# Plain fp32 products for layer 0's projections in a new order, and five changed joints between stages, in a two-layer encoder kernel

## What is computed

```python
for l in range(2):
    xn = rmsnorm(x, norm1_g[l])
    cq, ckv, k_rope, u, gate_a, gate_b = split(xn @ w_in[l])   # 256, 128, 32, 512, 1024, 1024 columns
    gate_a, gate_b = sigmoid(gate_a), sigmoid(gate_b)
    attn = mla(cq, ckv, k_rope)       # latent attention, 8 heads, q and k RMS-normed per head
    branch_a = attn @ w_attn_up[l]
    y = s5_bidir(u, ...)              # diagonal complex state space, 32 groups of 16 channels, both directions
    z = gelu(y) @ w_glu[l]
    branch_b = z[..., :1024] * sigmoid(z[..., 1024:])
    x = x + (gate_a * branch_a + gate_b * branch_b) @ w_o[l]
    x = x + (silu(rmsnorm(x, norm2_g[l]) @ w_ffn_gate[l]) * (rmsnorm(x, norm2_g[l]) @ w_ffn_up[l])) @ w_ffn_down[l]
```

## Time and profile before

| what | value |
|---|---|
| median of 3 executions | 1662.17 us (1661.73 to 1666.11) |
| profiled execution, its time | 1664.14 us |
| profiled execution, span of the trace | 1662.4 us |
| granted TensorE clock, mean | 0.969 |
| PE busy | 1544.8 us (93%) |
| DVE busy | 907.0 us (55%) |
| POOL busy | 587.1 us (35%) |
| ACT busy | 565.2 us (34%) |

### The profile page before, as it was taken

One profiled execution on the slowest core, in us unless ns is written; L12 is line 12 of the kernel. 1 busy time (PEld: TensorE's weight loads), 2 busy tenths in 40 slices (PEclk: granted clock), 3 DMA queues, 4 the chain that ended last, 5 costly groups with the idle time before them and its releaser, 6 DMA issues.

```text
span 1662.4 us, 21281 instructions
## 1 busy us (share of the span) xinstructions
PE 1544.8 (93%) x8488; PEld 1269.3 (76%) x8488; DVE 907.0 (55%) x1247; ACT 565.2 (34%) x885; POOL 587.1 (35%) x285
## 2 busy tenths in 40 slices
PE   6869598999999979999999799888999999999999
PEld 4757487777778858887888788777777788888887
DVE  7999677758645978683232643477593322112210
ACT  5322125663244222323232222467323322223220
POOL 3300013225444345433543322323344444444442
PEclk9979798999999989999999799999999999999999
DMA  5258650022233234535325462100332222222232
GB/s 183 89 170 283 212 216 19 2 77 92 86 107 111 76 127 149 198 95 167 104 99 181 170 238 71 64 1 27 102 99 79 90 101 98 93 90 91 98 102 76
DMA packets 73058, 188.36 MB, mean 113 GB/s; under 512 B 23552, under 2 KB 32000, under 8 KB 68864
## 3 DMA queue, kind: packets, MB, share of 16 engines
q1 hardware_dynamic: 35856, 124.99, 22.4%
q10 hardware_dynamic: 37104, 62.01, 11.3%
HBM read 154.47 MB, written 32.51 MB: 112 GB/s over the span
## 4 chain that ended last, share of the span: by engine, by line
PE 66%; DVE 19%; DVEq 5%; DMA 4%; ACT 3%; issue 2%; ACTq 1%; SPq 0%
PE ps L1413 21%; PE ps L1415 20%; PE ps L1414 20%; DVE mix L1356 2%; PE ps L1539 2%; DVE qkTl L1277 1%; DVE mix L1354 1%; DMA ctd_scr<-CPp 1%; DVE work L871 1%; DVE nmx L1310 1%; PE ps L1668 1%; ACT prob L783 1%; DMA y_scr<-SS 1%; PE ps L1677 1%; DVE work L872 1%
## 5 line engine op out<-in xcount | busy, mean ns | idle before, releaser
L392 POOL TENSOR_TENSOR wl<-stage,wh 128x1024 fp32r<-128x1024 f32 x215 | 538.7, 2510 | 930.4 <-ACT wh L456 930.3
L456 ACT ACTIVATE wh<-stage 128x1024 fp32r<-128x1024 f32 x228 | 239.2, 1055 | 394.1 <-PE ps L1415 259.2
L1413 PE MATMUL ps<-xg2h,wh 128*128 128x512 f32 x704 | 280.5, 398 | 2.6 <-DVE act L1385 2.6
L1414 PE MATMUL ps<-xg2l,wh 128*128 128x512 f32 x704 | 279.1, 396 | 0.0
L1415 PE MATMUL ps<-xg2h,wl 128*128 128x512 f32 x704 | 278.9, 396 | 0.0
L1413 PEld LDWEIGHTS ps<-xg2h,wh 128*128 128x128 f32 x704 | 132.6, 188 | 35.7 <-issue 3.9
L1415 PEld LDWEIGHTS ps<-xg2h,wl 128*128 128x128 f32 x704 | 132.7, 188 | 32.2
L1414 PEld LDWEIGHTS ps<-xg2l,wh 128*128 128x128 f32 x704 | 132.7, 188 | 32.1 <-issue 0.5
L1413 PE MATMUL ps<-xgh,wh 128*128 128x512 f32 x320 | 133.3, 416 | 19.0 <-DVE xgl L884 14.5
L1413 PE MATMUL ps<-hidh,wh 128*128 128x512 f32 x352 | 140.2, 398 | 0.0
L1415 PE MATMUL ps<-hidh,wl 128*128 128x512 f32 x352 | 139.4, 396 | 0.0
(11 more groups left out here) (264 smaller groups left out, 2837.2 us busy)
## 6 DMA issues: line engine op xcount, KB each, us to landing
stage<-in_stream SPq DMA_DIRECT2D x228, 512.0 KB, 3.3
CPTR<-ctd_scr ACTq DMA_DIRECT2D x8, 1664.0 KB, 8.9
ctd_scr<-CPp ACTq DMA_DIRECT2D x8, 1152.0 KB, 7.6
in_scr<-BPI ACTq DMA_DIRECT2D x8, 1024.0 KB, 4.9
InT<-in_scr ACTq DMA_DIRECT2D x8, 1024.0 KB, 5.1
ctd_scr<-TRa ACTq DMA_DIRECT2D x4, 1024.0 KB, 5.4
toep_scr<-Kf ACTq DMA_DIRECT2D x64, 64.0 KB, 2.8
Toep<-toep_scr ACTq DMA_DIRECT2D x8, 512.0 KB, 10.8
```

What stands on the lines that cost most here:

```text
L392: pool.tensor_tensor(wl[:, s, :], stage[:, s % STAGES, :], wh[:, s, :].bitcast(F32), ALU.subtract).then_inc(wl_ready, 1)
L456: return act.activation(o, i, ACT.Copy, **kw)
L1413: pe.matmul(o, wt[0], x[0], start=start, stop=False)
L1414: pe.matmul(o, wt[0], x[1], start=False, stop=False)
```

## The change

Six things are changed. (1) In layer 0's projections (slabs 0 to 23) PE multiplies unsplit fp32 slabs by `xg32`, x times the gain, in one matmul call per product instead of three. The slabs go to a ring of eight (`slabs`, in the memory of `wh` and `wl`), SP loads them ahead in a new order, ACT's splits and POOL's and DVE's remainders begin only at slab 24, and DVE makes `xg32` in one operation per row block. BPI of layer 0 has two buffers. The gates, taps, turned maps, powers, states and outputs of layer 0 stand in a new order on PE, DVE and ACT. (2) At layer 1's start ACT loads the maps of block 1 right behind those of block 0, and DVE does `states(0)` and gate 0 before the latents. (3) The q, k, v stage uses eight PSUM banks, and freeing a slab waits for ACT's copies and no longer for DVE's squares. (4) The gelu splits are made two at the second and two at the third attention-up pair. (5) The first two W_o tiles do products k = 0 to 6 each, then k = 7 of both. (6) `PREP_AT` is one step later.

```diff
-BY_VECTOR = range(S_GATE + 3, S_ATT)
-PREP_AT = tuple(8 + 4 * b for b in range(BLOCKS))
+RAW = S_ATT
+PREP_AT = tuple(9 + 4 * b for b in range(BLOCKS))
...
+RAWS = 2 * RING
...
+        slabs = nc.alloc_sbuf_tensor_at("slabs", [P, RAWS, 1024], F32, offset=ring_at)
...
+        xg32 = r.take("xg32", [P, KT, SEQ])
+        BPI = [[r.take(f"BPI0{i}", [P, 2, C8, P]) for i in range(2)]]
...
-        TURN_FIRST = ((0, 6), (2, 7), (1, 2), (3, 3))
+        TURN_FIRST = ((0, 4), (2, 5), (1, 6), (3, 7))
+
+        def qkv_bank(i):
+            return (4 + i) % 8
...
+            def raw(n):
+                if n >= RAWS:
+                    sp.wait_ge(slab_done, RING + n - RAWS + 1)
+                sp.dma_start(raw_slab(n), stream[n]).then_inc(raw_loaded[n % RAWS], 16)
+
             for k in range(KT):
+                if k in (0, 5):
+                    raw(k // 4)
                 sp.dma_start(X[:, k, :], xT[k]).then_inc(x_loaded[k], 16)
-                if k == 1:
-                    sp.dma_start(stage[:, 1, :], stream[1]).then_inc(staged[1], 16)
+                if k == 3:
                     sp.dma_start(par[0][:], params[0]).then_inc(par_loaded, 16)
-            sp.dma_start(Call[0][:].rearrange("p b r c -> p (b r c)"), cmat[0]).then_inc(call_loaded, 16)
+            raw(2)
             for src, dst in ((ident_in, identm[:]), (dskip, dsk[:].rearrange("p a g -> p (a g)")), (rope, csb[:].rearrange("p a t h -> p (a t h)"))):
                 sp.dma_start(dst, src).then_inc(const_loaded, 16)
-            for g in range(STAGES, DEPTH * SLABS):
-                sp.wait_ge(wl_ready, g - STAGES + 1)
+            sp.dma_start(Call[0][:].rearrange("p b r c -> p (b r c)"), cmat[0]).then_inc(call_loaded, 16)
+            for n in range(3, RAW):
+                raw(n)
+            for g in range(RAW, DEPTH * SLABS):
+                if g >= RAW + STAGES:
+                    sp.wait_ge(wl_ready, g - STAGES + 1 - RAW)
                 sp.dma_start(stage[:, g % STAGES, :], stream[g]).then_inc(staged[g % STAGES], 16)
...
                     act.wait_ge(xg_ready, KT * l + KT)
                     load_maps(l, 0)
+                    load_maps(l, 1)
...
-                    load_block(l, 1)
+                    load_u(l, 1)
...
+                    dve.wait_ge(col_loaded, 16)
+                    for k in range(KT + 1):
+                        if k < KT:
+                            dve.wait_ge(x_loaded[k], 16)
+                            ts(xg32[:, k, :], X[:, k, :], gcol[:, k:k + 1], None, MUL).then_inc(xl_ready, 1)
+                        if k:
+                            summed_x(l, k - 1)
+                    angles(0)
                     scales(0)
                 dve.wait_ge(rms_ready, 2 * l + 1)
...
-                            turns(0, (1, 2))
-                        if j == 3:
-                            turns(0, (4, 8, 16))
+                            input_powers(0, 0, 0)
...
+                    input_powers(0, 3, 1)
                     turns(0, (32,))
-                    for b in range(BLOCKS):
-                        input_powers(0, b, 0)
-                        gate(3 * b)
-                        remainder(S_GATE + 3 + 3 * b)
-                        if b:
-                            direct_taps(0, b - 1)
-                        else:
-                            latents()
-                        input_powers(0, b, 1)
-                        output_powers(0, b, 0)
-                        gate(3 * b + 1)
-                        remainder(S_GATE + 3 + 3 * b + 1)
-                        output_powers(0, b, 1)
-                        gate(3 * b + 2)
-                        remainder(S_GATE + 3 + 3 * b + 2)
-                        if b == 3:
-                            remainder(S_GATE + 15)
+                    gate(5)
+                    output_powers(0, 3, 0)
+                    direct_taps(0, 2)
+                    output_powers(0, 3, 1)
+                    gate(6)
+                    gate(7)
                     direct_taps(0, 3)
-                    dve.wait_ge(in_stored, 16 * BLOCKS)
+                    gate(8)
                     states(0)
+                    gate(9)
+                    gate(10)
+                    gate(11)
+                    states(1)
                     gate(12)
-                    states(1)
+                    states(2)
                     gate(13)
-                    states(2)
+                    states(3)
                     gate(14)
-                    states(3)
-                    gate(15)
                     for c in range(LC):
                         turned_latents(c)
+                    gate(15)
                 else:
-                    latents()
                     states(0)
                     gate(0)
+                    latents()
                     gate(1)
...
+                def gelu_split(i):
+                    dve.wait_ge(gelu_ready, BLOCKS * l + i + 1)
+                    cp(gyh[:, i, :], gel[:, i % 2, :])
+                    dve.drain()
+                    tt(gyl[:, i, :], gel[:, i % 2, :], gyh[:, i, :].bitcast(F32), SUB).then_inc(gy_ready, 1)
+
...
-                    dve.wait_ge(gelu_ready, BLOCKS * l + j + 1)
-                    cp(gyh[:, j, :], gel[:, j % 2, :])
-                    dve.drain()
-                    tt(gyl[:, j, :], gel[:, j % 2, :], gyh[:, j, :].bitcast(F32), SUB).then_inc(gy_ready, 1)
+                    if j in (1, 2):
+                        gelu_split(2 * j - 2)
+                        gelu_split(2 * j - 1)
...
+                def projected(o, n, k, start, stop):
+                    if l == 0:
+                        return pe.matmul(o, raw_slab(n)[:, k * P:(k + 1) * P], xg32[:, k, :], start=start, stop=stop)
+                    return products(o, weight(l, n, k * P, P), (xgh[:, k, :], xgl[:, k, :]), start, stop)
...
-                    if i >= 4:
-                        pe.wait_ge(qk_sq, PAIRS * TT * l + i - 3)
-                        if t == 3:
-                            pe.sem_inc(slab_done, 1)
+                    if i >= 8:
+                        pe.wait_ge(qk_sq, PAIRS * TT * l + i - 7)
+                    if i >= 4 and t == 3:
+                        pe.wait_ge(qkv_copied, PAIRS * TT * l + i - 3)
+                        pe.sem_inc(slab_done, 1)
                     wp = [w[:, (SLABS * l + S_ATT + hp) % RING, :] for w in (wh, wl)]
...
-                pe.wait_ge(qk_sq, PAIRS * TT * (l + 1))
+                pe.wait_ge(qkv_copied, PAIRS * TT * (l + 1))
                 pe.sem_inc(slab_done, 1)
+                pe.wait_ge(qk_sq, PAIRS * TT * (l + 1) - 4)
                 turn(0, 0)
                 turn(0, 1)
+                pe.wait_ge(qk_sq, PAIRS * TT * (l + 1))
                 for a in range(STEPS + 3):
...
+                def out_product(j, k):
+                    if j == 0:
+                        pe.wait_ge(mix_ready, KT * l + k + 1)
+                    return products(ps[:, j % 4, :], weight(l, S_WO + j, k * P, P), (mixh[:, k, :], mixl[:, k, :]),
+                                    k == 0, k == KT - 1)
+
+                for j in range(2):
+                    ready(S_WO + j)
+                    pe.wait_ge(xm_ready, KT * l + j + 1)
+                    for k in range(KT - 1):
+                        out_product(j, k)
+                for j in range(2):
+                    out_product(j, KT - 1).then_inc(slab_done, 1)
+                for j in range(2, KT):
+                    ready(S_WO + j)
+                    pe.wait_ge(xm_ready, KT * l + j + 1)
+                    for k in range(KT):
+                        last = out_product(j, k)
+                    last.then_inc(slab_done, 1)
```

More of the change, by code:

```diff
@@ L175, in build @@
         ffn_top = XGB + 4 * SEQ * (2 * HB + 7)
-        rot, pwc, pwi, BB, Call, Kf, work, BPI, CPp, par, small, pwr, TRa = ([] for _ in range(13))
+        rot, pwc, pwi, BB, Call, Kf, work, CPp, par, small, pwr, TRa = ([] for _ in range(12))
         for l in range(DEPTH):
@@ new lines, in _ @@
+                    gate_out(7)
+                    taps(0, 3)
+                    store_taps(0, 3)
+                    gate_out(8)
+                    for i in range(2):
+                        act.wait_ge(in_stored[i], 32)
+                    act.wait_ge(cp_stored, 16 * BLOCKS)
+                    act.wait_ge(k_stored, 128 * BLOCKS)
+                    load_block(0, 1)
+                    gate_out(9)
+                    gate_out(10)
+                    output_y(0, 0)
+                    gate_out(11)
```

260 lines of the change are left out of this document (144 added, 116 removed).

## The result

The changed kernel took a median of 1641.45 us over 4 executions (1639.71 to 1644.64), the kernel before 1664.1 us on the same occasions; the ratio is 0.9869, with a 95% interval of 0.9853 to 0.9886. That is 1.3% or 22 us less. 48 were forecast, and 1641 lies just outside the range, which ended at 1638. The profiled execution took 1644.64 us.

The account below looks back on a forecast made before the run. PE, busy 93% of the span, was taken as the bound, with DVE binding early in layer 0. Terms -18 - 6 - 4 - 4.8 - 7 - 8.4 = -48.2 took the median from 1662.2 to 1614 us; range 1597 to 1638.

Parts of the forecast that it names:

- PE's price of an unsplit product: Layer 0's projections: 0.86 us a product against 0.70 for three split matmuls, 26 us more over 160 products.
- Rival C: Slower than before: weight loads of fp32 products are not hidden, 1.24 us a product, total 1675 us; chance .05.
- rival A: Layer 0 gives only -2 to -6: a product costs 0.93 us, or the clock stays low in new gaps; 1630, chance .20.
- What DVE sheds: Layer 0: 13 remainders go, 15 us of DVE; without POOL's work, 11 stretches of about 2.1 us go too.
- the start: Layer 0's start: reciprocal near 26.5 us instead of 38.02, 11.5 us sooner; u tiles' last take at 47.9, done at 48.8.
- DVE's chain up to gate 6: Layer 0: DVE's work sums to 83.5 us, so DVE takes gate 6 near 132.5 and is still the bound.
- The rest of layer 0: Layer 0 from gate 8: a chain of 16.5 us a block, ending at 230.3 instead of 249.57; -18 us.
- Change 2: Layer 1's start: U wait and clock around it gained, states sooner, double map load costing 8 us; -6, ends -12 and +1.
- Rival B: Layer 1's double map load makes U so late that states(0) is no sooner; total 1621 us, chance .10.
- Change 3: q, k, v: eight banks remove two waits of 2.5 us and the half clock behind; -4 for both layers, ends -1 and -5.
- Changes 4 and 5: GLU: waits of 2.4 us twice go, -4.8; W_o: 3.5 us a layer from other products at hand, -7.
- Change 6: Layer 0's feed-forward: preparing a step later removes nearly all of DVE's and PE's wait; -8.4, ends -5 and -9.4.

Follow-up runs that it names:

- filled_waits: The changed kernel with unread fp32 products in PE's waits for S (layer 0 blocks 1 and 2, layer 1 block 0): 1642.4 us, ratio 0.9868.
- inputs_first: The changed kernel with inputs(b+1) ahead of outputs(b) at layer 0's tail, as in the kernel before: 1628.2 us, ratio 0.9786.
- late_maps: The changed kernel with layer 1's maps of block 1 loaded behind U of block 0: 1637.0 us, ratio 0.9833.
- orders_only: The changed kernel with the orders of inputs_first and late_maps, nothing unread in it: 1623.5 us, ratio 0.9741.
- prep_undone: The changed kernel with PREP_AT at 8 + 4b and the turned states' store at step 8, as before: 1645.3 us, ratio 0.9894.
- gate_2_first: late_maps with gate 2 taken on DVE ahead of states(1) in layer 1: 1640.8 us, ratio 0.9852.
- all_together: inputs_first, late_maps and gate_2_first in one kernel, plus five unread products ahead of each layer's first scores: 1623.1 us, ratio 0.9756.
- all_filled: all_together plus five unread products each in layer 1's wait for U (block 1) and ahead of layer 0's gate 11: 1611.9 us, ratio 0.9673.
- prep_10: The changed kernel with PREP_AT at 10 + 4b, the store moved to step 9: 1646.2 us, ratio 0.9891.

## Why the prediction was wrong, and where it was right

*What bounds the kernel:* right. The gain came from fewer waits of PE, and it was smaller because waits moved and because PE's own work grew by 34 us in layer 0.

*PE's price of an unsplit product:* right, 0.87 for a forecast of 0.86. The Trainium skill's page "FP8 and Floating Point Precision", section "TensorE Precision Notes", says that true fp32 makes four passes through the array. At the 0.233 us at which split matmuls start that would be an estimate of 0.93 us; the trace has 0.87, nearer to four passes than to three (0.70). Rival C falls, and so does rival A's first cause.

*What DVE sheds, the start, DVE's chain up to gate 6:* right within 1 us at 27.1 and 48.5; gate 8 had to wait for gate 6's take until 134.0 (forecast 132.5). DVE's long operations vanished there together with POOL's work, and in layer 1 of the changed kernel, where POOL works again, they are back: 2.93 and 2.69 us for operations that take 0.68 and 0.69 elsewhere.

```profile
925.07 2.93 DVE L1204 TENSOR_TENSOR RV<-RT,CPTR 128x512 f32<-128x512 f32 x1
928.07 2.69 DVE L1206 TENSOR_TENSOR RT<-RT,CPTR 128x512 f32<-128x512 f32 x1
925.04 5.16 POOL L417 TENSOR_TENSOR wl<-stage,wh 128x1024 fp32r<-128x1024 f32 x2 [2.87 <-ACT wh L477]
```

The Trainium skill's page "SBUF — State Buffer", section "Who interferes with whom", says that the port pair which DVE and GpSimd share is an exclusive lock; these rows agree.

*The rest of layer 0:* here the prediction failed, in two terms. "I take off 1.5 for a slower clock": four rows at the half clock alone cost 9.7 us. And the chain "inputs, states, the memory part of the outputs" was put in at 16.5 a block (its terms make 16.3) without a price for the order that makes it a chain, which is 13 us. The outputs of block 0 ended at 179.7, not 173.5; the gates behind PE's three waits of 2.3 to 4.5 us took 8.5 to 8.8 us in place of 7.1, and U came 1.2 us late. From there to the end 10.9 us more were lost. Outputs of blocks 1 and 2 took 7.1 in place of 3.8, twice, inputs 3.6 in place of 2.1, twice: 9.7 us. S came 10.8 and 11.6 us behind the end of the inputs, for my 10.6. filled_waits shows it from the other side: the same rows at full clock, and 7.8 us back in its trace, though not in its median. Clock: 0.83 from 200 to 247 us. The forecast 16.5 us a block was 19.8 and 22.1. I had even priced L1539 as half of a row at the half clock, and did not ask what had put it there. The comparison with the order of before was missing too: there a block took 13.75 us:

```profile
214.56 2.08 PE L1516 MATMUL ps<-U,InT 128*64 128x64 f32 x64
228.31 2.08 PE L1516 MATMUL ps<-U,InT 128*64 128x64 f32 x64 [0.22 <-DMA InT<-in_scr]
```

Had I set the two side by side, 13 us for one swap would have been a term of its own: with the swap undone (inputs_first) layer 0 ends at 233.8, 15.8 us sooner than before, near the -18. This is rival A by its second cause, a clock that stays low in the new gaps, together with the order, which no rival named: layer 0 gave -2.2, within its -2 to -6.

*Change 2:* wrong in size. The store's wait was 18.3 us against my 7.55 + 8 = 15.6, PE waited 3.6 + 2.8 (forecast 5). But a wait of 3.8 us for S and the half clock came behind them, so "gained: the 6.68 us wait and the clock around it" failed. The stage came out just past my range's edge, +1.1 for +1. Rival B has the result and not the cause: it said that states(0) is no sooner, and they began 52.4 us into the stage, before 58.3. But they took 19.0 us (916.05 to 935.05), before 12.7, as three more of their operations stood beside POOL's, the two above among them, and PE waited for the last one:

```profile
935.11 7.09 PE L1604 MATMUL ps<-S,CPTR 64*128 64x64 f32 x64 [3.81 <-DVE S L1217]
```

That stretching was no term of the prediction. late_maps, where states(0) took 12.8 us again, shows the double load's price, 5 us: the stage took 177.6 and in orders_only 174.8, 4 to 7 us under the kernel before, around the forecast -6.

*Change 3:* mis-sized. The waits and "what follows at half clock" were counted as gained; the chain of DVE ends when it did, PE's waits add up to the same 12 us, and the clock is the same 0.80. 1.5 to 1.7 in place of 4.

*Changes 4 and 5:* right in the mechanism. Both waits are gone and nothing took their place, as PE has other products at hand. Change 5 gave -7.2 for -7. Change 4 gave -6.8 for -4.8, outside its ends of -3 and -5.5: the sum had only the wait of 2.4 us a layer, and in layer 1 slower products stood behind it too (granted clock 0.57 from 1196 to 1200 us).

*Change 6:* wrong in "so nearly all of the wait is gone". I had counted PE's distance from the store, not the work that moves into DVE's freed time. -2.8 between the traces, -4.6 by prep_undone, for -8.4.

*The signs:* the product's pace, DVE's operations and the reciprocal came as said. q, k, v began at 247.4 (near 230), PE waited 3.45 us at L1480 (not over 1), and the second u tile was held 10.8 us longer than before (some 8), with the inputs of block 0 8.4 us later in the stage; the prediction's own mark for being wrong was a hold of over 10. The clock of layer 0 was 0.93, above its mark of 0.85, and 0.83 only at the end.

The range was too narrow since the misses are not independent: in layer 0, layer 1's start and q, k, v alike a wait of PE remained or moved, and the half clock behind it was not in the sum.

What stays open: why the clock comes back after some microseconds in one kernel and only after 20 in another behind much the same wait for U. late_maps and orders_only (4.0 and 4.1 us) were at half clock for 3 us, gate_2_first and all_together (4.6 and 4.0) for 20. No run here tells that.

## What to carry to other kernels

Price a wait of TensorE as the wait plus the slower work behind it, and look in the trace at the same engine's rows after the waits that will remain, not after the ones that go: here, by the traces, a wait of 2 to 5 us cost 3 to 11 us more. Add up the waits of a stage before and after: a change that only gathers them saves nothing. Issue the input of the next block ahead of the output of this one where a slower engine stands between them: here that was 13 us. When a wait can't be removed, compare with useless products in it, in both orders, before giving up an order as worthless.

## What the runs showed of the hardware

Useless work made the kernel faster: 4.4 us of unread products in one wait took 11 us off layer 1's stage and 9 us off the total (1640.8 to 1631.8); between all_together and all_filled the same filling went with 8 us off that stage. A stretch in which PE was busy for every microsecond was granted a clock of 0.50 for 10 us behind a wait of 4.6 us. And two kernels with the same work in layer 0 reached q, k, v at 238.2 and 241.9 us after their first product (prep_10, gate_2_first), so about 4 us of a stage's time is chance and not change. Part of it lies in the clock: from 190 to 230 us the changed kernel was granted 0.63, 0.86, 0.65 and 0.67 in its four windows of 10 us and late_maps 0.77, 0.89, 0.80 and 0.86, and q, k, v began at 247.4 and 244.9 us.
